# Two attentions of a two-block decoder kernel: the projections between values, scores, turning and output are divided at weight pieces

## The reference, cut to what matters

```python
h = x @ w_in[l]
(hg_q, hg_f, hg_i, hg_gate, mla_cq, mla_ckv, mla_kr, mla_gate, mem_q, mem_gate) = split(h)
y_hg  = hgrn2(hg_q, hg_f, hg_i)                     # gated recurrence, 8 heads
y_mla = latent_attention(mla_cq, mla_ckv, mla_kr)   # causal, 8 heads, in two groups of 4
y_mem = softmax(q k^T / sqrt(128)) v                # 4 heads, keys and values from mem
y = concat([y_hg * silu(hg_gate), y_mla * silu(mla_gate), y_mem * silu(mem_gate)])
x = layernorm(ALPHA * x + y @ w_out[l])
```

## Time and profile before

| what | value |
|---|---|
| median of three runs | 1194.95 us (1194.27 to 1195.27) |
| profiled execution, its own time | 1196.89 us |
| its span, first to last instruction | 1195.1 us |
| TensorE busy (matmul) | 1075.3 us, 90% of the span |
| VectorE busy | 733.9 us, 61% |
| ScalarE busy | 661.2 us, 55% |
| mean granted TensorE clock | 0.957 of full speed |

### The profile page before, as it was taken

One profiled execution on the slowest core, in us unless ns is written; L12 is line 12 of the kernel. 1 busy time (PEld: TensorE's weight loads), 2 busy tenths in 40 slices (PEclk: granted clock), 3 DMA queues, 4 the chain that ended last, 5 costly groups with the idle time before them and its releaser, 6 DMA issues.

```text
span 1195.1 us, 19133 instructions
## 1 busy us (share of the span) xinstructions
PE 1075.3 (90%) x8070; PEld 949.7 (79%) x8070; DVE 733.9 (61%) x1093; ACT 661.2 (55%) x926; POOL 43.3 (4%) x50
## 2 busy tenths in 40 slices
PE   1699999999999999998999987888999998988884
PEld 1589988888879999887989976576889898855763
DVE  1566667775555878754556456865675555667563
ACT  3666656564464556543655578327446565783360
POOL 1000000000000000000000001310000000013100
PEclk9999998999998999998999999879999999989897
DMA  7446234556455565574545434013565454240220
GB/s 251 146 141 211 86 111 157 175 167 191 157 158 183 170 207 164 197 215 129 160 125 163 133 128 141 2 30 116 173 198 159 123 186 142 71 141 2 73 88 35
DMA packets 97656, 167.53 MB, mean 140 GB/s; under 512 B 7000, under 2 KB 32482, under 8 KB 97314
## 3 DMA queue, kind: packets, MB, share of 16 engines
q1 hardware_dynamic: 94912, 157.08, 41.5%
q0 software_dynamic: 1472, 5.51, 1.4%
q10 hardware_dynamic: 1186, 3.72, 0.8%
HBM read 165.23 MB, written 1.05 MB: 139 GB/s over the span
## 4 chain that ended last, share of the span: by engine, by line
PE 75%; DVE 12%; ACT 8%; issue 3%; DMA 1%; ACTq 1%; DVEq 0%
PE proj L540 11%; PE proj L549 10%; PE proj L541 10%; PE proj L542 10%; PE proj L550 10%; PE proj L551 10%; DVE wlo L1238 2%; ACT whi L895 1%; PE mix L821 1%; DVE arena L462 1%; DMA arena<-in_mem 1%; DVE arena L463 1%; PE mix L851 1%; PE mix L568 1%; PE mix L560 1%
## 5 line engine op out<-in xcount | busy, mean ns | idle before, releaser
L1238 DVE TENSOR_TENSOR wlo<-raw,whi 128x1024 fp32r<-128x1024 f32 (+3 forms) x303 | 354.8, 1202 | 205.4 <-ACT whi L895 204.6
L895 ACT ACTIVATE whi<-raw 128x1024 fp32r<-128x1024 f32 (+3 forms) x303 | 305.3, 1041 | 233.7 <-PE proj L542 110.0
L540 PE MATMUL proj<-act_hi,whi 128*128 128x256 f32 x1056 | 304.7, 289 | 6.7 <-DVE act_lo L1259 3.4
L541 PE MATMUL proj<-act_lo,whi 128*128 128x256 f32 x1056 | 302.0, 286 | 0.0
L542 PE MATMUL proj<-act_hi,wlo 128*128 128x256 f32 x1056 | 301.8, 286 | 0.0
L540 PEld LDWEIGHTS proj<-act_hi,whi 128*128 128x128 f32 x1056 | 206.1, 195 | 8.0 <-DVE act_lo L1259 3.6
L541 PEld LDWEIGHTS proj<-act_lo,whi 128*128 128x128 f32 x1056 | 206.2, 195 | 0.2
L542 PEld LDWEIGHTS proj<-act_hi,wlo 128*128 128x128 f32 x1056 | 205.9, 195 | 0.0
L549 PE MATMUL proj<-whi,y_hi 128*128 128x512 f32 (+1 forms) x352 | 140.6, 399 | 22.6 <-DVE y_lo L1259 9.5
L550 PE MATMUL proj<-wlo,y_hi 128*128 128x512 f32 (+1 forms) x352 | 138.5, 393 | 0.0
L551 PE MATMUL proj<-whi,y_lo 128*128 128x512 f32 (+1 forms) x352 | 138.2, 393 | 0.0
(11 more groups left out here) (330 smaller groups left out, 1285.2 us busy)
## 6 DMA issues: line engine op xcount, KB each, us to landing
raw<-in_w_in SPq DMA_DIRECT2D x144, 512.0 KB, 4.4
raw<-in_w_up SPq DMA_DIRECT2D x88, 256.0 KB, 3.9
raw<-in_w_out SPq DMA_DIRECT2D x32, 512.0 KB, 4.7
raw<-in_w_down SPq DMA_DIRECT2D x22, 512.0 KB, 5.1
raw<-in_w_mem_kv SPq DMA_DIRECT2D x8, 512.0 KB, 5.6
raw<-in_w_mem_k SPq DMA_DIRECT2D x8, 512.0 KB, 4.0
raw<-in_w_o SPq DMA_DIRECT2D x8, 512.0 KB, 4.4
raw<-in_w_mem_v SPq DMA_DIRECT2D x8, 512.0 KB, 3.5
```

Source lines behind the costliest of these rows:

```text
L540: mm(o, wh[:, i, wc], hi[:, k0 + i, :], start=begin and j % 2 == 0, stop=False, skip_group_check=True)
L541: mm(o, wh[:, i, wc], lo[:, k0 + i, :], start=False, stop=False, skip_group_check=True)
L895: fn(whi[c % SPLIT][:, 0:w], raw[c % SLOTS][:, 0:w], ACT.Copy).then_inc(s.w_hi, 1)
L1238: tt(wlo[c % SPLIT][:, 0:w], raw[c % SLOTS][:, 0:w], f32(whi[c % SPLIT][:, 0:w]), ALU.subtract).then_inc(s.w_lo, 1)
```

## The change

`project` can now run a part of a group's pieces (`part=(from, to)`); it waits for the PSUM tensor only with the first. An argument `half` comes with it that nothing uses. In the memory attention the values are put between the second and third piece of `mlag`. In the latent attention the last piece of `hgf1` moves behind the turning of group 0, the first piece of `hgg0` ahead of the scores of group 1, and the first piece of `hgi0` ahead of the values of group 1. ScalarE and VectorE split fewer pieces at these places, and ScalarE takes `mlag` and `hgf1` out later.

```diff
-            def project(name, L, hi, lo, tile0=0, ready=None):
+            def project(name, L, hi, lo, tile0=0, ready=None, part=None, half=None):
                 g, ps, c0 = place[L, name], shape[L, name], first[L, name]
-                if g >= 2:
+                begin_at, end_at = part or (0, len(ps))
+                if g >= 2 and begin_at == 0:
                     pe.wait_ge(evac[g % 2], g // 2)
...
-                k0 = tile0
-                seen = 0
-                for n, loads in enumerate(ps):
+                seen = sum(piece_dims(loads)[0] for loads in ps[:begin_at])
+                k0 = tile0 + seen
+                for n in range(begin_at, end_at):
+                    loads = ps[n]
...
 # TensorE
                 attend_turn(1 + L, MP)
-                project("mlag", L, act_hi, act_lo)
+                project("mlag", L, act_hi, act_lo, part=(0, 2))
                 attend_values(1 + L, lambda m, h: MV[:, m, h * P:(h + 1) * P], MPT)
+                project("mlag", L, act_hi, act_lo, part=(2, 4))
                 pe.wait_ge(*stage(2, L))
...
-                for grp, more in enumerate(("hgf1", "hgg0")):
+                for grp, (more, begin, then, close) in enumerate((("hgf1", 0, "hgf1", 3), ("hgg0", 1, "hgi0", 0))):
                     if grp:
+                        project("hgg0", L, act_hi, act_lo, part=(0, 1))
                         pe.wait_ge(s.mla_yl, L + 1)
...
-                    project(more, L, act_hi, act_lo)
+                    project(more, L, act_hi, act_lo, part=(begin, begin + 3))
                     pe.wait_ge(s.mla_p, 2 * L + grp + 1)
...
                     last.then_inc(s.mla_pt, 1)
+                    project(then, L, act_hi, act_lo, part=(close, close + 1))
                     pe.wait_ge(s.mla_ptk, 2 * L + grp + 1)
...
-                project("hgi0", L, act_hi, act_lo)
+                project("hgi0", L, act_hi, act_lo, part=(1, 4))
 # ScalarE
                 attend_turned(1 + L, MPT)
+                split_until(first[L, "mlag"] + 2 + SPLIT - 1)
+                attend_out(1 + L, MP, 0, True)
                 leave("mlag", L, LGT, ACT.Silu)
-                attend_out(1 + L, MP, 0, True)
...
                     if grp == 0:
-                        leave("hgf1", L, HF[:, 4:8, :])
+                        split_until(first[L, "hgf1"] + 3 + SPLIT - 1)
                     else:
                         leave("hgg0", L, HGT[:, 0:4, :], ACT.Silu)
                     act.wait_ge(s.mla_pt, 2 * L + grp + 1)
                     fn(LPT, mix[:, 0:4, 0:TRI], ACT.Copy).then_inc(s.mla_ptk, 1)
+                    if grp == 0:
+                        leave("hgf1", L, HF[:, 4:8, :])
 # VectorE
                 attend_shares(1 + L, MP, XA_D ** -0.5)
-                for name in ("ckv", "mlag"):
-                    split_until(pieces_until(name, L))
+                split_until(first[L, "mlag"] + 2 + SPLIT - 1)
...
-                    split_until(pieces_until("hgg0" if grp else "hgf1", L))
+                    split_until(pieces_until("hgg0", L) if grp else first[L, "hgf1"] + 3 + SPLIT - 1)
```

More of the change, by code:

```diff
@@ L551, in project @@
                                 last = mm(o, lo[:, k0 + i, tb], wh[:, i, :], start=False, stop=end)
+                            if half is not None and n == len(ps) - 1 and b == 0:
+                                last.then_inc(half, 1)
                     last.then_inc(s.w_used, 1)
```

## The result

Over 20 runs each the changed kernel takes 1201.22 us in the median (1194.37 to 1203.81), the kernel before 1193.88 (1188.60 to 1196.37). The ratio is 1.006, 95% interval 1.0046 to 1.0075: slower, by 7.3 us. Beside later experiments the change ran again and gave 1.0067 (1.0044 to 1.009). The forecast was slower by 4.3 us, at 1199.3 us, range 1196.2 to 1203.2.

What follows compares the result with a forecast made beforehand. TensorE, busy 90%, was taken as the bound, so only its gaps could be won. Layer 0 (3.35 + 0.63 - 1.66), layer 1 (3.57 - 1.66) and 0.1 gave +4.3 us: 1199.3 us, range 1196.2 to 1203.2.

Steps and rivals of the forecast that it cites:

- mechanism: Latent attention, group 1: a postponed split delays a load; ScalarE's in-order queue then holds back the copy and the values.
- likeliest case: Whole kernel: memory attention gains, late load delays group 1's values; 4.3 us slower, 1197.8 to 1201 us, 58%.
- case C: Rival, group 1: load lands 5 us after issue and both slow stretches cost in full; 1203.1 us, 15%.
- both slow stretches: TensorE at slower clock behind group 1's gap (0.63 us booked, layer 0) and in `hgi1` (0.1 for both layers).
- Case A: Rival, group 1: the raw buffer is free in time, so the copy isn't starved; 1189.7 us, faster, 12%.
- Q: First piece of `hgi0`; forecast split late, at 704.6 to 705.85, freeing the raw buffer for the first piece of `hgi1`.
- Memory attention: Wait ahead of `memout0` goes, about 1.1 us appears ahead of `hgq0`; 1.66 us won per layer.
- Values of group 1: Latent attention: values start later behind the late load; 3.35 us lost in layer 0, 3.57 in layer 1.
- landing of R: Load of the first piece of `hgi1`, group 1: lands 3.6 us after issue, bounds 3.5 to 6.3.
- Behind the values: Step from group 1's values to `decays`: 0.63 us for a slower clock in layer 0, to near 32.3 us.
- 0.1 for `hgi1`: Second slow stretch behind a gap in `hgi1`: 0 to 0.6 us per layer possible, 0.1 taken for both.
- Case B: Rival, memory attention: the addition ahead of `hgq0` isn't late, 2.8 us won per layer; 1197.0 us, 13%.

Runs made afterwards that it cites:

- Q late: Kernels where VectorE splits the first piece of `hgi0` only behind the shares of group 1, as the whole change does; the change itself measured 1.006.
- latent alone: Latent attention's part of the change only, memory attention as in the kernel before: 1203.85 us, ratio 1.0093.
- before with Q late: Undivided kernel before, with only VectorE's run of splits in group 0 ended one piece sooner: 1205.94 us, ratio 1.0118.
- memory alone: Memory attention's part of the change only, latent attention as in the kernel before: 1189.05 us, ratio 0.9976.
- memory alone, adds: Memory attention's part only, with VectorE's two postponed splits made before its wait for ScalarE's root: 1187.09 us, ratio 0.995.
- Q in time: Whole change, but VectorE splits the first piece of `hgi0` in group 0 as the kernel before did: 1189.64 us, ratio 0.9984.
- adds in time: Q in time, plus VectorE making the memory attention's two postponed splits before waiting for ScalarE's root: 1187.48 us, ratio 0.9953.
- copy ahead: Adds in time, plus ScalarE copying group 1's turned shares before it takes `hgg0` out: 1184.38 us, ratio 0.9936.
- gap filled: Whole change plus 36 extra TensorE transposes per layer ahead of the first piece of `hgi0`: 1201.6 us, ratio 1.007.

## Why the prediction was right, and where it was too small

**Sign, mechanism and range: right.** The median of 1201.22 lies in the range, but 0.2 us above the end of the range given for the likeliest case alone (1197.8 to 1201). The time came out nearer than the loss, by luck: the forecast stood on a median of 1194.95 from three runs, and over 20 runs it is 1193.88, so 1199.3 was 1.9 us too low, but the loss of 4.3 against 7.3 was 3.0 too low. What the traces show lies between the likeliest case and case C, which had 15%: layer 0 has a landing of 5.0 us and both slow stretches in full, as C has it, layer 1 the landing of the likeliest case and the first slow stretch. Every wait named was there: none ahead of `memout0`, 0.88 us ahead of `hgq0` (1.1 worked out), 0.82 and 1.13 us ahead of the turnings (0.9 and 1.2), none in group 0 for the copy and `mla_yl`, over 5 us ahead of the values of group 1, and ScalarE's fourth split standing for its load. Case A needed Q split in time, which the change doesn't do; the run of that name does.

**Memory attention: right.** 1.66 us per layer worked out, 1.62 and 1.58 in the trace, 2.5 in the medians of the part alone against 3.3.

**Values of group 1: right in layer 1, too small in layer 0.** The step from `hgq0` to them grew by 3.63 us in layer 1 (3.57 worked out), by 4.74 in layer 0 (3.35). The term at fault is the landing of R. I took 3.6 us from the earlier trace rows for both layers, as the first load on an idle queue, near the lower end of the earlier trace rows. The kernel before had a nearer row in the same trace: the first load behind the splits of group 1 (issued at 706.7 in layer 0, at 1029.9 in layer 1) took 4.0 and 3.6 us. In the changed kernel it took 5.0 in layer 0 (above); in layer 1, tile raw from 1030 to 1031.5 us:

```profile
DMA to landing us min/median/max: 3.6/3.6/3.6
```

The difference is 1.4 us, inside the bound of the earlier trace rows. It is no accident of one execution: in the six traces with Q late R lands in 3.9 to 5.1 us in layer 0 and in 3.5 or 3.6 in layer 1. Why layer 0's load lands later I can't say; no run was made for it.

Two readings ahead of it were off by 0.1 us or less and change nothing: from 703.30 to 705.50 are 2.20 us, not 2.15, and from 709.0 to 714.3 are 5.3, not 5.2.

**Behind the values: too small in both.** I booked 0.63 us for a slower clock, in layer 0 only, and 0.1 for `hgi1`. The trace has +2.30 and +0.69. The stretches of the changed kernel, behind the values of layer 0, around the wait in `hgi1` of layer 0, and behind the values of layer 1:

```profile
710.40:713.40 3.00, 3.00 (x17) 2.03 (x18) 0.11 (x1) 0.00 (x0) 0.00 (x0) 0.50 0.16 61
727.00:731.00 4.00, 2.79 (x7) 2.21 (x8) 4.00 (x4) 3.98 (x5) 0.00 (x0) 0.53 0.40 120
1038.90:1041.90 3.00, 3.00 (x17) 2.03 (x18) 0.08 (x1) 0.00 (x0) 0.00 (x0) 0.50 0.26 101
```

Behind the long gap the clock is at half for all three microseconds, where the earlier trace rows have 0.62 over four. In seven of the eight layers with a gap of over 5 us (the change twice, latent alone, before with Q late) the step is 32.95 to 32.98 instead of 31.65: 1.3 us, not 0.63, since layer 1 of before, which I measured the surcharge from, had a shorter slow phase. That row was also less firm than I took it: gaps of the same length left the clock where it was, or didn't. Behind 2.93 us (memory alone, layer 0) and behind 2.94 us (memory alone, adds, layer 1) the next three microseconds are

```profile
707.50:710.50 3.00, 3.00 (x23) 2.39 (x24) 0.72 (x2) 0.63 (x1) 0.00 (x0) 1.00 0.94 339
1026.60:1029.60 3.00, 2.95 (x17) 2.13 (x18) 0.36 (x1) 0.00 (x0) 0.00 (x0) 0.57 0.97 363
```

with steps to `decays` of 31.66 and 32.64 us.

The eighth layer is layer 0 of the first trace of the change, with 33.95; the further microsecond there goes with the second slow phase, behind the wait of 3.70 us in `hgi1`: its 0 to 0.6 us per layer in my bound was too little. The other traces bear this out. Behind seven waits of 3.83 to 3.85 us in `hgi1` (Q in time, adds in time, copy ahead, layer 1 of the gap filled) the clock fell each time; where it stayed at 0.50 for five microseconds the step is 32.67, 32.32 and 32.60 us, where it rose sooner (0.66 to 0.71 over the five) it is 31.64 or 31.65.

Together: 1.4 for the landing, 1.7 and 0.6 behind the values, 0.2 from the smaller differences, 3.9 us on top of the 4.3 forecast, which is the 8.2 of the steps; the medians have 7.3. The mechanism was right, and two terms were mis-sized, both on the same side: for the landing I took one of the shortest in the trace, and for the slow phase the one row there was, behind a gap little more than half as long as the one forecast.

That the half clock adds to the loss is read from the traces. The run that was to show it by itself didn't: with the gap filled the time didn't fall. How much of the loss would go with an always full clock stays open.

**Case B** (the addition not late) was an outcome that didn't come, but names what the change left lying: with the two splits moved, `hgq0` comes 1.2 us sooner per layer.

## What to carry to other kernels

Where a loader waits for a consumer's progress, a split that is postponed by one piece postpones a load as many pieces on as there are buffers (four here), and the load then appears on another engine, in another group, in front of work that has nothing to do with it. So before the points are moved to which each engine prepares its pieces, follow each postponed split to the load that it frees and to whatever stands behind that load on an in-order engine. Put short copies that a busy engine waits for ahead of preparatory work, and preparatory work ahead of waits: here three such edits took the ratio to before from 1.006 to 0.9936.

## What the runs showed of the hardware

- A gap ahead of TensorE's work cost more than itself here. Behind the eight gaps of 5.2 us and more ahead of the values the next three microseconds ran at half clock (0.50), and the step that follows grew by 1.3 us in seven of them, by 2.3 in the eighth. Behind gaps up to 1.55 us the clock stayed at 1.00. In between equal gaps ended either way: 1.00 behind 1.95 and 2.93 us, 0.53 behind 2.05 and 0.57 behind 2.94.
- The same load of 512 KB, the first behind a pause of the queue, lands 3.6 us after its issue in one layer and 5.0 in the other, with the same order of instructions around it. Over the six traces with Q late it took 3.9, 4.3, 4.4, 5.0, 5.1 and 5.1 us in layer 0, and 3.5 or 3.6 in layer 1.
- The slow phases fall differently from run to run: the same kernel before took 1188.6 to 1196.4 us, and the trace of the change was 3.7 us ahead of that of before at a point ahead of which both do the same.
